# A streaming encoder step on one core: both attentions move from stages of their own into pieces between the expert slots, and the stick-breaking suffix sums accumulate on the logits in PSUM

## The chip, the cores and the metric

One core of one Trainium2 chip (trn2), all arithmetic in fp32. The metric is the device time of one execution in microseconds (us). Engines: PE is TensorE's matmul, PEld its weight load, DVE is VectorE, ACT is ScalarE, POOL is GpSimd, SP is SyncE, which here only issues transfers.

## The reference

1024 prompt rows (8 tiles of 128) and 8 x 16 sample rows (a ninth tile), width 1024. Per layer, cut to what matters:

```
h = rmsnorm(x);  q, k, v, gates = h @ w_in
o_sb  = stick-breaking attention, 8 heads x 64:
          log_keep    = where(mask, -softplus(z), 0)
          log_between = reverse cumsum(log_keep) - log_keep
          weight      = where(mask, exp(log_sigmoid(z) + log_between), 0)
o_sw  = sliding-window softmax, 8 query / 2 key heads x 64, sinks, ALiBi
o_mem = softmax over 256 memory tokens, 4 heads x 128
x += (sum_b gate_b * (o_b @ w_o_b)) @ w_out
x += experts(rmsnorm(x)):  8 heads x top 16 of 16384 single-neuron experts,
       sum over 128 slots of g * gelu(u[idx] . x) * v[idx]
```

The sample tile also attends to caches: 128 past rows of keys and values per sequence for both attentions, and 256 memory rows.

## The kernel before

It has four blocks with a barrier between them. Line numbers are those of the profile.

`project` (lines 81 to 427) normalises the tiles, multiplies them with eight blocks of weights (ksb, vsb, kvsw, qsw, qm, mk, mv, qsb) and leaves queries, keys and values of all nine tiles in SBUF. SP issues the weight loads and the outputs in one written order; a load waits for the block two before it.

`stick` (430 to 672) is the stick-breaking attention: 38 steps, one for each pair of a query tile and a key tile up to the diagonal, and two for the samples. A step is 1024 columns wide (8 heads x 128). PE writes the logits to PSUM; ACT takes Abs, a copy, Exp and Ln (590 to 595), DVE makes the softplus (637), POOL keeps the running sum `later` (612), PE multiplies the softplus by a triangle and `later` by minus ones (531, 533), DVE adds that to the copied logits (651), ACT takes the Exp (581), PE multiplies with the values (552). Line 574 names one activation table set by hand ahead of it, `natural_log_exp_and_others`.

`windows` (675 to 938) is the sliding-window and the memory attention: 27 units (9 tiles, two key heads and the memory), each a softmax over 4 x 256 columns, three in flight. The sample tile's cached keys are transposed on PE there. Outputs of both attentions go to a scratch in DRAM.

`experts` (1020 to 1645) works tile by tile through 128 slots: POOL gathers 128 rows of 8 KB for each slot (1254) into a ring of ten; two slots are a batch (64 a tile, 576 in all). For a batch DVE takes two dot products (1618), ACT the Gelu (1457), DVE the product `wgt` (1624), ACT the diagonal matrices (1468), and PE adds two products of 512 columns to the accumulator (1375). Of tiles with a number in `SIDES`, that many slots of eight go to POOL instead: ACT scales the row (1473) and POOL adds it (1265). Between the batches every engine also does pieces of the `Front` of the next group of tiles: gates and output projections (1298, 1308, tanh 1403, mix 1564), `w_out` (1323), the norm, the expert queries (1346), the key scores (1360), and for the group's first tile the top-k (1489 to 1513) in three pieces a head; the top-k of a later tile is done between the batches of the tile ahead of it. `Front` gives each kind of piece its steps (tau); `paces()` spreads the steps of the next front over the batches of the present group, and `advance(i)` lets each engine do the steps of batch i. Every engine runs its own instructions in the order written, so a piece that waits holds up the batch behind it. Before the first tile, the front of group 0 runs alone up to its first head. The groups are tiles 0 to 1, 2 to 4 and 5 to 8.

```
for q in range(NB):                                   # ScalarE, one batch
    act.wait_ge(dots, m * NB + q + 1)
    nc.scalar.activation(act_[:, c], hid[:, c], ACT.Gelu_apprx_tanh).then_inc(gelus, 1)
    advance(1 + m * NB + q)
    act.wait_ge(weights, m * NB + q + 1)
    ...
```

## Time and profile before

| | us |
|---|---|
| median of 3 runs (4420.18 to 4424.81) | 4423.85 |
| the profiled execution, its own time | 4421.1 |
| its span, first to last instruction | 4419.2 |
| before the first expert slot | 1147 |
| the expert slots of the nine tiles | 3272 |

The span is what the views divide up; the profiled execution's own time is 1.9 us longer. PEclk is TensorE's granted clock as a share of 2.4 GHz. A stretch is named by its first and last microsecond from the span's start. The first tile starts at 1147 us with line 1610.

### The profile page before, as it was taken

Reading aid. Unit: us, or ns where it says so; the run is one execution under the profiler, and the core shown is the slowest. Engines: PE = TensorE matmul, PEld = TensorE weight load, DVE = VectorE, ACT = ScalarE, POOL = GpSimd, SP = SyncE. Lnnn points to the kernel's source line nnn. Section 1 sums busy time; section 2 is a strip of 40 time slices with the busy share of each in tenths; the row PEclk is TensorE's granted clock in tenths of the full one; section 3 lists DMA queues with packets and bytes.
Section 4 is the critical chain, followed back from the end, with each engine's and each line's share of the span. In section 5 each row is a group of like instructions: output and inputs, shape, how many; then the busy total and the mean of one; then the engine's idle time right before and its main releaser. Section 6 shows DMA issues by size and latency. Waiting matters only on the chain.

```text
span 4419.2 us, 34952 instructions
## 1 busy us (share of the span) xinstructions
PE 3611.0 (82%) x11113; PEld 1885.0 (43%) x11113; DVE 2811.9 (64%) x6038; ACT 1235.3 (28%) x2663; POOL 1836.7 (42%) x1477
## 2 busy tenths in 40 slices
PE   7999798989768797867898878996787777787777
PEld 4545457778534345432333335442233233233222
DVE  2130541821698965886996997687677676676554
ACT  2111772620332233332223224333111112112111
POOL 0000340000366576656666666666433333333332
PEclk9999996989889999988999999998899999999999
DMA  3202102234799899989999999999999999999998
GB/s 123 69 25 80 30 1 86 84 122 162 293 351 391 319 405 421 396 333 421 421 419 421 412 420 415 422 411 409 421 421 421 417 412 418 415 413 414 421 421 354
DMA packets 249160, 1415.44 MB, mean 320 GB/s; under 512 B 26624, under 2 KB 59648, under 8 KB 95872
## 3 DMA queue, kind: packets, MB, share of 16 engines
q0 software_dynamic: 165888, 1208.03, 66.6%
q1 hardware_dynamic: 83088, 205.18, 12.6%
q8 instruction: 88, 1.44, 0.1%
q14 instruction: 96, 0.79, 0.0%
HBM read 1374.85 MB, written 39.19 MB: 320 GB/s over the span
## 4 chain that ended last, share of the span: by engine, by line
DMA 23%; POOL 18%; DVE 13%; PE 12%; issue 11%; ACT 2%; POOLq 0%; SPq 0%; ACTq 0%; DVEq 0%
DMA ring<-in_experts_dram,idx 22%; POOL side L1265 10%; POOL ring L1254 8%; PE ps L1375 7%; DVE ring L1618 5%; PE ps L1298 2%; PE ps L1323 1%; DVE wgt L1624 1%; PE ps L1346 1%; PE ps L1308 1%; ACT diag L1468 1%; DVE hot L1507 1%; DVE hot L1510 1%; DVE e L1512 1%; DVE flat L1503 0%
## 5 line engine op out<-in xcount | busy, mean ns | idle before, releaser
L1375 PE MATMUL ps<-ring,diag 128*128 128x512 f32 x3520 | 1792.9, 654 | 688.4 <-ACT diag L1468 667.1
L1254 POOL DMA_INDIRECT ring<-in_experts_dram,idx x1152 | 1096.1, 952 | 1905.9 <-PE ps L1375 1334.5
L1618 DVE CUSTOM_DVE_ANT_0 ring<-ring,ps 128x1024 f32<-128x1024 f32 x1152 | 1381.7, 1217 | 556.1 <-DMA ring<-in_experts_dram,idx 548.7
L1375 PEld LDWEIGHTS ps<-ring,diag 128*128 128x128 f32 x3520 | 695.3, 206 | 1693.2 <-ACT diag L1468 948.7
L1265 POOL TENSOR_TENSOR side<-side,ring 128x1024 f32<-128x1024 f32 x272 | 640.8, 2356 | 42.6 <-ACT ring L1473 37.4
L1457 ACT ACTIVATE act_<-hid 128x2 f32<-128x2 f32 x576 | 117.1, 203 | 1773.5 <-DVE hid L1618 1772.8
L1468 ACT ACTIVATE diag<-const,wgt 128x128 f32<-128x128 f32 x880 | 319.4, 395 | 482.8 <-DVE wgt L1624 480.2
L1298 PE MATMUL ps<-hx,wbuf 128*128 128x256 f32 (+2 forms) x1152 | 403.1, 495 | 13.3 <-DMA hx<-hT_scratch 13.1
L1624 DVE TENSOR_TENSOR wgt<-act_,gw 128x2 f32<-128x2 f32 x576 | 240.9, 418 | 124.9 <-ACT act_ L1457 121.6
L1473 ACT ACTIVATE ring<-ring,wgt 128x1024 f32<-128x1024 f32 x272 | 308.4, 1134 | 0.0
L1298 PEld LDWEIGHTS ps<-hx,wbuf 128*128 128x128 f32 x1152 | 225.6, 196 | 184.5 <-issue 119.3
L301 PE MATMUL ps<-w_qkv,hT 128*128 128x512 f32 (+1 forms) x720 | 283.5, 550 | 1.3 <-DVE mhT L395 1.3
L1346 PE MATMUL ps<-hx,wbuf 128*128 128x256 f32 (+2 forms) x768 | 264.4, 493 | 12.2 <-ACT mixn L1426 11.0
L610 POOL COPY later<-sp 128x1024 f32<-128x1024 f32 x9 | 9.3, 1036 | 478.9 <-DVE sp L643 475.5
L1346 PEld LDWEIGHTS ps<-hx,wbuf 128*128 128x128 f32 x768 | 149.7, 196 | 129.7 <-issue 96.3
L1308 PE MATMUL ps<-o_x,wbuf 128*128 128x256 f32 (+2 forms) x576 | 204.1, 491 | 0.0
L301 PEld LDWEIGHTS ps<-w_qkv,hT 128*128 128x128 f32 x720 | 134.1, 190 | 131.0 <-issue 125.4
L637 DVE SCALAR_TENSOR_TENSOR sp<-ps,za 128x1024 f32<-128x1024 f32 x38 | 46.5, 1224 | 193.2 <-ACT za L595 193.2
L404 DVE TENSOR_REDUCE nrm<-stage 128x4 f32<-128x512 f32 (+2 forms) x29 | 16.3, 561 | 237.9 <-ACT stage L347 237.9
L1308 PEld LDWEIGHTS ps<-o_x,wbuf 128*128 128x128 f32 x576 | 111.4, 193 | 84.4 <-issue 58.5
L1323 PE MATMUL ps<-wbuf,mixn 128*128 128x256 f32 x576 | 129.8, 382 | 1.6 <-DVE mixn L1564 1.6
L1323 PEld LDWEIGHTS ps<-wbuf,mixn 128*128 128x128 f32 x576 | 110.6, 192 | 29.0 <-issue 15.1
(187 smaller groups left out, 3096.6 us busy)
## 6 DMA issues: line engine op xcount, KB each, us to landing
wbuf<-in_w_gate_o_dram SPq DMA_DIRECT2D x72, 768.0 KB, 8.3
wbuf<-in_w_q_dram SPq DMA_DIRECT2D x24, 1024.0 KB, 9.0
ring<-in_experts_dram,idx POOLq DMA_INDIRECT x1152, 16.0
wbuf<-in_w_out_dram SPq DMA_DIRECT2D x12, 1024.0 KB, 8.9
w_qkv<-in_w_in_dram SPq DMA_DIRECT2D x5, 2048.0 KB, 8.0
o_x<-o_scratch SPq DMA_DIRECT2D x9, 768.0 KB, 25.2
s<-s_scratch SPq DMA_DIRECT2D x6, 1024.0 KB, 11.6
hT_scratch<-hT SPq DMA_DIRECT2D x9, 512.0 KB, 7.0
```

The lines of the kernel that those rows point to most:

```text
L301: last = nc.tensor.matmul(ps[:, bank(u), 0:n], src[:, k, t * P:(t + 1) * P], w[:, c % 2, k, 0:n], start=(k == 0), stop=(k == KC - 1))
L1254: i = nc.gpsimd.indirect_dma_start(out=ring[:, j % RING, :], out_offset=None, in_=A["experts"], in_offset=bass.IndirectOffsetOnAxis(ap=idx ...
L1265: nc.gpsimd.tensor_tensor(side[:, m % 2], side[:, m % 2], ring[:, j % RING, DM:2 * DM], ALU.add).then_inc(side_done, 1)
L1298: last = nc.tensor.matmul(ps[:, 4 + u % 2, 0:N].rearrange("p (i t) -> p i t", t=P), w[:, k * P:(k + 1) * P], hx[:, 0:n, k, :], start=(k == ...
L1308: last = nc.tensor.matmul(ps[:, 6 + u % 2, 0:N].rearrange("p (i t) -> p i t", t=P), w[:, k * P:(k + 1) * P], o[:, 0:n, b, k - KC, :], star ...
L1323: last = nc.tensor.matmul(ps[:, 4 + x % 4, 0:2 * P], mixn[:, k * N + i * P:k * N + (i + 1) * P], w[:, k * 2 * P:(k + 1) * 2 * P], start=(k ...
L1346: last = nc.tensor.matmul(ps[:, 4 + x % 2, 0:N].rearrange("p (i t) -> p i t", t=P), w[:, c:c + P], hx[:, 0:n, k, :], start=(k == 0), stop= ...
L1375: last = nc.tensor.matmul(acc[:, h, :], diag[:, (by_pe(j) - 1) % 4, :], ring[:, j % RING, DM + h * HB:DM + (h + 1) * HB], start=(j % SLOTS ...
L1468: last = nc.scalar.activation(diag[:, d % 4, :], ident, ACT.Copy, scale=wgt[:, j % SLOTS:j % SLOTS + 1])
L1473: nc.scalar.activation(v, v, ACT.Copy, scale=wgt[:, j % SLOTS:j % SLOTS + 1]).then_inc(scaled, 1)
L1618: last = nc.vector.tensor_tensor_reduce(out=u, in0=u, in1=xp, scale=1.0, scalar=0.0, op0=ALU.mult, op1=ALU.add, accum_out=hid[:, j % SLOTS ...
L1624: nc.vector.tensor_tensor(wgt[:, c], act_[:, c], gw[:, m % 2, c], ALU.mult).then_inc(weights, 1)
```

## The change

`stick` and `windows` go. `project` also writes everything that they took from SBUF to scratches in DRAM: the normalised rows (nine transfers of 512 KB, before in `stick`), keys, values and three kinds of queries, and the memory's. `Front` now begins with the attentions of its own group and goes on with the gates. Groups are three tiles each. The stick-breaking steps are halves of 512 columns (four heads); group 0 has 12, group 1 has 30, group 2 has 34. Their logits stay in one of three PSUM banks, and the suffix sums are accumulated onto them there, so that the copy (591) and the add (651) go; `later` is kept on DVE instead of POOL. The window units have one set of PSUM banks instead of two. Keys and values come in again a step at a time through rings of three; the bias, the window's and the memory's keys and values come in when the group's stick-breaking part is done, and the gate weights and `hx` when its windows are done, since all of them share one working area. The caches' keys are given to the kernel already transposed. The hand-named table set goes. Steps have costs, and `paces()` spreads the costs, at most two steps a batch. `advance` moves ahead of the accumulation on PE, and behind `wgt` and the diagonals on DVE and ACT. Tiles 2 to 5 now give four slots of eight to POOL (before three in tiles 2 to 4, none in tile 5).

With the numbers of the file, group 0's front runs alone for 136 steps, to its first head, and ends at batch 22 of tile 0. Group 1's stick-breaking steps take batch 22 of tile 0 to batch 3 of tile 1 (46 batches, 29 of which compute logits, one of them of two halves), its windows go on to batch 18 of tile 1, its gates to batch 11 of tile 2, the rest to batch 55 of tile 2. Group 2's stick-breaking steps take batches 0 to 52 of tile 3 (53 batches, 34 with logits), its windows go on to batch 16 of tile 4, its gates to batch 10 of tile 5, the rest to batch 55 of tile 5.

```diff
-GROUPS = ((0, 1), (2, 3, 4), (5, 6, 7, 8))
-PARTS = (2, 3, 4)
-SIDES = (4, 4, 3, 3, 3, 0, 0, 0, 0)
+GROUPS = ((0, 1, 2), (3, 4, 5), (6, 7, 8))
+PARTS = (2, 3, 3)
+SIDES = (4, 4, 4, 4, 4, 4, 0, 0, 0)
 def project(nc, A, S, small_dram, D):
...
+                for t in range(NT):
+                    if kind == "ksb":
+                        sp.dma_start(D["k"][t].rearrange("p (j t) -> p j t", j=4), cols("ksbT", t)).then_inc(spilled, 16)
+                    elif kind == "vsb":
...
+                if t == 1 and c >= 1:
+                    ns += spill(c - 1)
+                if t == 4 and c == 0:
+                    sp.wait_ge(h_done, NX)
+                    for i in range(NT):
+                        sp.dma_start(D["hT"][i], hT[:, :, i * P:(i + 1) * P]).then_inc(spilled, 16)
+                    ns += NT
...
-def stick(nc, A, S, hT_d):
...
-def windows(nc, A, S, wide_dram, o_d):
...
 class Front:
...
+        self.steps_ = []
+        b = 1
+        for i, t in enumerate(GROUPS[g]):
+            kbs = list(range(t, -1, -1)) if t < ST else [ST, None]
+            for k, kb in enumerate(kbs):
+                self.steps_.append((i, t, kb, k == 0, k == len(kbs) - 1, b))
+                b += 2
...
+        self.zscore, self.soft, self.suffix, self.values = at(0), at(1), at(2), at(6)
+        self.plain = at(2, lambda x: not x[3])
+        self.least, self.dexp, self.mask = (at(lag, lambda x: x[3]) for lag in (2, 3, 4))
+        self.late = at(3, lambda x: not x[4])
+        self.okeep = {x[5] + 8: k for k, x in enumerate(self.steps_) if x[4]}
...
+                self.wins.append((i, t, c, b))
+                b += 2 if c < 2 else 3
...
+        self.wscore, self.wfront, self.wexp, self.wnorm = wat(0), wat(1), wat(2), wat(3)
+        self.wturn = {x[3] + 4 + k: (u, k) for u, x in enumerate(self.wins) for k in range(2)}
+        self.wvalues, self.wkeep = wat(6), wat(7)
...
+            c = 0.8
+            c += 4.5 * (tau in self.zscore or tau in self.suffix)
+            c += 2.0 * (self.win_at + 2 <= tau < self.gate_at)
+            c += 10.3 * n / 4 / Y * (tau in self.unit)
+            c += 3.5 * (tau in self.out)
+            c += 3.4 * n / 4 * (tau in self.query) + 1.0 * (tau in self.top)
...
 def paces():
...
+            goal = total * min(1.0, (i + 1) / (ticks - 8))
+            n = 0
+            while at < len(left) and (n < 2 and spent + left[at] / 2 <= goal or i >= ticks - 9):
+                spent += left[at]
+                at += 1
+                n += 1
+            out.append(n)
...
         @block.sync
...
+                    if tau in f.zscore:
+                        k, p = f.zscore[tau]
+                        if p == 1 and k + 3 < f.nkeys:
+                            sp.wait_ge(z_done, f.half(k, 1) + 1)
...
+                    if tau == f.win_at:
+                        sp.wait_ge(st_kept, f.tiles0 + n)
+                        sp.dma_start(bias.rearrange("p h k -> p (h k)"), wide_dram[:, 0:BW]).then_inc(bias_in, 16)
+                        first = 0 if g else 1
+                        for src, dst in ((0, kswT), (1, vsw)):
+                            v = sw_d[f.base - 1 + first:f.base + n, :, src].rearrange("t p c -> p t c")
+                            sp.dma_start(dst[:, first:n + 1], v).then_inc(win_in, 16)
+                        sp.dma_start(mkT.rearrange("p h m -> p (h m)"), mem_d[:, 0]).then_inc(win_in, 16)
+                        sp.dma_start(mv.rearrange("p k m -> p (k m)"), mem_d[:, 1]).then_inc(win_in, 16)
...
+                    if tau in f.mul:
+                        k = f.mul[tau]
+                        for b in range(2 * k + 2, 2 * k + 4):
+                            sp.wait_ge(mul_done, b - 1)
+                            if b < DB:
+                                sp.dma_start(kmem[:, b % 2], A["cache_mem_kT"][b]).then_inc(km_in[b % 2], 16)
+                            else:
+                                load_vm(b - DB)
...
+                    if tau == f.gate_at:
+                        sp.wait_ge(w_kept, f.win1)
+                        for i in range(2):
+                            load(f, i)
+                        for i in range(n):
+                            sp.dma_start(hx[:, i], hT_d[f.base + i]).then_inc(h_in, 16)
...
         @block.tensor
...
+                            pe.wait_ge(minned if f.steps_[k3][3] else weighed, f.sort(k3, p3) + 1)
...
+                        pe.wait_ge(sp_ready, x + 1)
+                        z = ps[:, 4 + x % 3, :]
+                        last = nc.tensor.matmul(z, tri, sps[:, x % 3], start=False, stop=True, skip_group_check=True)
+                        if not first:
+                            pe.wait_ge(latered, f.lates(k - 1, p) + 1)
+                            last = nc.tensor.matmul(z, negones, later[:, p], start=False, stop=True, skip_group_check=True)
+                        last.then_inc(sums, 1)
...
             for m in range(NT):
                 for q in range(NB):
-                    if q == 0:
-                        advance(1 + m * NB)
+                    advance(1 + m * NB + q)
                     accumulate(m, q)
-                    if q:
-                        advance(1 + m * NB + q)
...
         @block.scalar
...
+                        a = za[:, x % 2]
+                        nc.scalar.activation(a, ps[:, 4 + x % 3, :], ACT.Abs).then_inc(absd, 1)
+                        act.wait_ge(absd, x + 1)
+                        nc.scalar.activation(a, a, ACT.Exp, scale=-1.0).then_inc(zexped, 1)
+                        act.wait_ge(zexped, x + 1)
+                        nc.scalar.activation(a, a, ACT.Ln, bias=1.0).then_inc(logd, 1)
+                    if tau in f.dexp:
+                        k, p = f.dexp[tau]
+                        w = wts[:, f.half(k, p) % 5]
+                        act.wait_ge(minned, f.sort(k, p) + 1)
+                        nc.scalar.activation(w, w, ACT.Exp).then_inc(dexped, 1)
+                    if tau in f.plain:
+                        k, p = f.plain[tau]
+                        x = f.half(k, p)
+                        act.wait_ge(sums, x + 1)
+                        if x >= 5:
...
                     nc.scalar.activation(act_[:, c], hid[:, c], ACT.Gelu_apprx_tanh).then_inc(gelus, 1)
-                    advance(1 + m * NB + q)
                     act.wait_ge(weights, m * NB + q + 1)
...
                             nc.scalar.activation(v, v, ACT.Copy, scale=wgt[:, j % SLOTS:j % SLOTS + 1]).then_inc(scaled, 1)
+                    advance(1 + m * NB + q)
...
         @block.vector
...
+                    if tau in f.least:
+                        k, p = f.least[tau]
+                        x = f.half(k, p)
+                        dve.wait_ge(sums, x + 1)
+                        if x >= 5:
+                            dve.wait_ge(pv, x - 4)
+                        nc.vector.tensor_scalar(wts[:, x % 5], ps[:, 4 + x % 3, :], 0.0, None, ALU.min).then_inc(minned, 1)
+                    if tau in f.late:
+                        k, p = f.late[tau]
+                        x = f.half(k, p)
+                        dve.wait_ge(sums, x + 1)
+                        if f.steps_[k][3]:
+                            nc.vector.tensor_copy(later[:, p], sps[:, x % 3]).then_inc(latered, 1)
+                        else:
+                            dve.wait_ge(latered, f.lates(k - 1, p) + 1)
+                            nc.vector.tensor_tensor(later[:, p], later[:, p], sps[:, x % 3], ALU.add).then_inc(latered, 1)
...
+                        sp_ = sps[:, x % 3]
+                        nc.vector.scalar_tensor_tensor(out=sp_, in0=ps[:, 4 + x % 3, :], scalar=0.0, in1=za[:, x % 2],
+                                                       op0=ALU.max, op1=ALU.add).then_inc(sp_raw, 1)
...
+    A["cache_kT"] = give("cache_kT", kc.reshape(DB, P, 4, 2, HD).transpose(3, 4, 0, 2, 1).reshape(P, DB, 4, P))
```

## Rows read from the trace of the kernel before

**Rows 1.** The page, part 1: busy us (share of the span) xinstructions of each engine.
```profile
PE 3611.0 (82%) x11113; PEld 1885.0 (43%) x11113; DVE 2811.9 (64%) x6038; ACT 1235.3 (28%) x2663; POOL 1836.7 (42%) x1477
```

**Rows 2.** Stretches before the first expert slot: us, engines' busy us, PEclk, DMA share, GB/s.
```profile
0.00:429.00 429.00, 402.63 (x1189) 214.41 (x1189) 83.05 (x189) 71.98 (x172) 0.55 (x6) 0.98 0.19 68
429.00:715.00 286.00, 246.68 (x1731) 150.59 (x1732) 122.48 (x102) 191.50 (x199) 99.19 (x47) 0.90 0.11 32
715.00:951.00 236.00, 204.73 (x1243) 182.01 (x1242) 119.78 (x210) 94.60 (x279) 0.00 (x0) 0.77 0.28 92
951.00:1080.00 129.00, 127.76 (x576) 111.10 (x576) 16.54 (x40) 12.87 (x26) 0.00 (x0) 0.98 0.48 165
1080.00:1118.00 38.00, 31.54 (x146) 27.35 (x147) 6.78 (x15) 5.92 (x9) 0.00 (x0) 0.96 0.61 211
1118.00:1147.00 29.00, 29.00 (x148) 25.85 (x147) 12.54 (x54) 6.40 (x13) 1.14 (x1) 1.00 0.46 156
```

**Rows 3.** The expert slots, one stretch for each tile: tiles 0 to 5, and 8.
```profile
1147.00:1600.00 453.00, 339.80 (x889) 178.34 (x888) 395.90 (x871) 140.88 (x255) 272.87 (x194) 0.88 0.92 359
1600.00:2024.00 424.00, 320.70 (x938) 174.86 (x936) 307.33 (x623) 137.24 (x259) 273.91 (x193) 0.91 0.97 392
2024.00:2376.00 352.00, 306.48 (x666) 130.30 (x667) 297.06 (x615) 103.28 (x210) 241.97 (x180) 0.95 1.01 420
2376.00:2741.00 365.00, 311.63 (x808) 157.01 (x806) 300.19 (x626) 105.52 (x213) 232.59 (x174) 0.94 1.01 416
2741.00:3103.00 362.00, 296.02 (x731) 134.26 (x731) 273.73 (x602) 125.86 (x252) 237.78 (x178) 0.89 1.01 415
3103.00:3431.00 328.00, 251.05 (x515) 101.67 (x513) 235.40 (x593) 61.11 (x196) 124.07 (x131) 0.93 1.01 421
...
4088.00:4419.00 331.00, 241.93 (x520) 94.09 (x520) 171.21 (x324) 58.12 (x195) 112.84 (x121) 0.99 0.96 399
```

**Rows 4.** Line 1624 alone, one a batch: us, busy us (batches), PEclk, DMA share, GB/s.
```profile
1328.00:1600.00 272.00, 30.81 (x40) 0.94 0.92 361
1801.00:1929.00 128.00, 14.20 (x16) 0.95 0.90 343
1608.00:1706.00 98.00, 15.21 (x16) 0.98 1.01 421
...
3107.00:3395.00 288.00, 9.03 (x56) 0.92 1.01 421
```

**Rows 5.** A transfer of 512 KB beside the expert slots: KB, median us to landing.
```profile
xrow<-xn_scratch SPq DMA_DIRECT2D x9, 512.0 KB, 11.3
```

**Rows 6.** Groups of instructions: xcount | busy us, mean ns | idle before. ScalarE.
```profile
L1468 ACT ACTIVATE diag<-const,wgt 128x128 f32<-128x128 f32 x880 | 319.4, 395 | 482.8 <-DVE wgt L1624 480.2 <-PE ps L1375 2.3
L1473 ACT ACTIVATE ring<-ring,wgt 128x1024 f32<-128x1024 f32 x272 | 308.4, 1134 | 0.0
L1457 ACT ACTIVATE act_<-hid 128x2 f32<-128x2 f32 x576 | 117.1, 203 | 1773.5 <-DVE hid L1618 1772.8
L355 ACT ACTIVATE vsb<-ps 128x512 f32<-128x512 f32 x9 | 5.4, 597 | 56.3 <-PE ps L301 56.3
```

**Rows 7.** ScalarE in order of time around an Exp between two other functions.
```profile
1140.88 1.28 ACT L1449 ACT_TABLE_LOAD   x1
1142.17 0.22 ACT L1449 ACTIVATE best<-best 128x16 f32<-128x16 f32 x1
1142.41 1.28 ACT L1457 ACT_TABLE_LOAD   x1
```

**Rows 8.** The view of rows 6, VectorE.
```profile
L1618 DVE CUSTOM_DVE_ANT_0 ring<-ring,ps 128x1024 f32<-128x1024 f32 x1152 | 1381.7, 1217 | 556.1 <-DMA ring<-in_experts_dram,idx 548.7 <-DVE idx L1513 1.4 <-DVE gw L1533 0.6
L637 DVE SCALAR_TENSOR_TENSOR sp<-ps,za 128x1024 f32<-128x1024 f32 x38 | 46.5, 1224 | 193.2 <-ACT za L595 193.2
```

**Rows 9.** Line 1624: duration ns min/median/max, first and last start.
```profile
L1624 DVE TENSOR_TENSOR wgt<-act_,gw x576: 146/160/2989, 1164.7 to 4410.3; 128x2 f32<-128x2 f32 x192
```

**Rows 10.** A stretch late in tile 1, in the columns of rows 3.
```profile
1929.00:2024.00 95.00, 45.58 (x77) 16.11 (x75) 70.51 (x141) 28.68 (x53) 62.64 (x44) 0.75 0.98 393
```

1071 lines of the change are left out of this document (528 added, 543 removed).

## The prediction

> **What bounds the kernel now.** PE is busy 82% of the span [rows 1], so I read where in the span, by stretches. Until 1147 us no expert is gathered: 429 us of projections, 286 of stick-breaking, 236 of windows, 196 of group 0's front, with the DMA share at 0.11 to 0.61 [rows 2]. Then nine tiles take 3272 us. From tile 2 on (tiles 6 and 7 are like tile 5) the DMA share reads 1.01 at 415 to 421 GB/s: gathers bound these tiles, and a batch without pieces costs 288 / 56 = 5.1 us [rows 3, 4]. Tiles 0 and 1 are not at that bound (0.92 and 0.97). Where pieces of the top-k and of the front meet, DVE sets the pace: 128 / 16 = 8.0 us a batch at 1801 to 1929 us, 272 / 40 = 6.8 at 1328 to 1600, against 6.1 at 1608 to 1706, where the DMA is full again [rows 4]. PE is seldom what ends last there: tile 2 took 352 us with 306 of PE. So the change moves work from a place where transfers are idle to one where they bound. It pays if the pieces fit under 5.1 to 5.7 us a batch, and one engine that doesn't fit stops all, since each works in order.
>
> **Before the first slot.** Projections, 429 us: the spill of the memory queries now stands in SP's order ahead of the last block's weights (8 us, about one landing of [rows 5]), the last nine spills follow the last product (11), and the first loads must land (11.3, of which some 2 were there): +28, between +10 and +45. The other spills lie under PE's work, at a DMA share of 0.19 [rows 2]. Without that cover their 19 MB would cost some 45 us.
>
> Stick-breaking of group 0, 12 halves: ACT takes four passes of 512 columns, 0.60 each [rows 6], and two table loads of 1.28 [rows 7], 5.0 in all. That gives 60, and the turns between three tiles 16: 76 us. At the old rate of 286 / 38 = 7.5 a step, six steps would be 45. That and 110 are the ends.
>
> Windows of group 0, nine units on one set of banks: product (2, my estimate), bias and maximum on DVE (1.22 each for 1024 columns [rows 8], plus 0.5 for small ones, an estimate), four Exp at 0.6 at most [rows 6]: 7.4 a unit, 67 for nine, 10 until the last is out, 11 for the loads [rows 5]: 88. A third of 236 would be 79; I keep up to 120.
>
> Gates to first head: three tiles in place of two. 129 x 1.5 = 194; the 38 grow to 52 (28 of it scale, 10 don't); the 29 to 38; and 11 for weights that are asked for only when the windows are done: 295.
>
> Sum: 457 + 76 + 88 + 295 = 916 where 1147 was, **-231 us**.
>
> **In the slots: stick-breaking.** Take ACT in a batch with one logits half. Gelu 0.20, one diagonal 0.40, one scaled row 1.13, Abs, Exp, Ln and the weights' Exp 0.60 each: 4.1 us [rows 6]. To that come table loads. In [rows 7] an Exp between two other functions cost two loads of 1.28, with 0.01 us between load and neighbour. The change runs Exp, Ln, Exp, Gelu in a circle and no longer names a table set. No row shows whether Exp and Ln then share a set. I take four loads, 5.1 us, because the kernel before had to name the joint set by hand; two is the other end. So 9.3 us, and a batch at a tile's start needs two or three loads: 8.7 on average, 8.4 in group 2. The next Gelu stands behind the pieces on ACT, `wgt` behind Gelu (0.15 to 2.99 us, [rows 9]) and the diagonals behind that, so about 0.6 of ACT's idle time comes on top: 9.3 and 9.1. DVE in such a batch has two dots (2.6 with their read-outs), `wgt` 0.5, a softplus and a `later` of half the 1.22 each with waits, 2: about 5 [rows 8], which is hidden, but with the third piece of a head's top-k (8) it is 13. The ring of ten covers five batches once, then the slow rate stands.
>
> Group 1: 46 batches, 29 x 9.3 + 17 x 5.6 + 8 heavy pieces x 4 = 397. Before, 46 x 6.8 = 313 [rows 4]. **+84**. Group 2: 53 batches, 34 x 9.1 + 19 x 5.6 + 32 = 448; before at tile 3's 365 / 64 = 5.7 [rows 3], 302. **+146**. The copy, the add and POOL's `later` that go were hidden in the old stage's time, already removed above.
>
> By the Trainium skill (ScalarE: Activation LUTs, What ACT_TABLE_LOAD costs) a switch also takes a drain and costs 2.66 us in all; the some 310 new loads would add 430 us to my sum. The trace disagrees with that part: [rows 7] leave no room for it.
>
> **Windows.** DVE's 5.3 us a unit (1.22 three times, a copy and small ones 1.6) x 9 = 48, over 15 batches 3.2, on 3.1 of the slots and 1.7 of the top-k: 8.0 against 6.1, +28. In group 2 over 28 batches 6.5 against 5.7, +22. The sample's 16 memory transfers go two deep: six times PE waits some 11 us [rows 5] in four or five batches, with `accumulate`, and behind it POOL's gathers, queued: +25, between 5 and 70. Window and gate loads start one batch ahead of use, four places, 11 less 6 each: +20.
>
> **The rest of the front** spreads further. Tile 5 had none (328); at tile 1's full-DMA rate of 6.1 [rows 4] it takes 378: +50. Tile 2 +30, tile 4 +20, tile 1 +5; tiles 6 to 8 as before. One more slot of eight on POOL in tiles 2 to 4, and four in tile 5, is in these rates: tile 1 ran so, with POOL at 274 of 424 [rows 3]. New bytes (keys, values, bias, caches, some 36 MB) are 86 us at 420 GB/s, but lie in batches that are now slower than the DMA.
>
> `advance` behind `wgt` and the diagonals takes the front's waits out of PE's way, but DVE and ACT do the same work in a batch: I take nothing, and 30 either way for the ends.
>
> Sum: 84 + 146 + 28 + 22 + 25 + 20 + 105 = **+430**. The profiled execution took 4421.1 (span 4419.2), 2.7 below the median of 4423.85, under 0.1%. 4421 - 231 + 430 = **4620 us**. A measurement of this kernel can tell about 0.2%, 9 us, from no change.
>
> **Rivals.**
> A. *Everything fits under the gathers* (the other side: faster). If a batch with stick-breaking comes to about 6 us, the ring evens it out and bytes alone bound the slots. That needs ACT's loads nearly gone. The nine slot stretches times their DMA shares are some 3210 (two are not shown) [rows 3]; with 86 of new bytes, 10 of start and 60 for tile 0's top-k, 3366; with 916, 4282. For it: 0.92 to 1.01 in [rows 3]. Against it: 4.1 us plus even two loads is 6.7. 0.14.
> B. *Two loads a batch.* The batch falls by 2.2 us in 63 batches, less where DVE's heavy pieces rule, 115; and group 0's halves need none, 31: 4474. For it: nothing in [rows 7] excludes it. The Trainium skill (ScalarE activation tables: per-element evaluation and per-set limits, Table sets in the compiler and the runtime) says that loads are placed by the greedy longest run, which would choose the joint set here; no run so far shows it. 0.2, with a quarter of it below 4412.
> C. *PE falls to its lower clock and the loads queue.* At full clock 288 products of 256 columns took 128 us [rows 2], 0.44 each, so 512 columns 0.87. A stick-breaking batch has 0.9 of logits, 0.9 of values, 1.7 of sums and 1.7 of accumulation, 5.2 us, half of a batch of 9.3. Half busy late in tile 1 (46 of 95 us, [rows 10]) the granted clock read 0.75. At 1.2 GHz it is 10.4, over ACT's 9.3: 63 x 1.5 = 95, and the load waits double, 45: 4760. 0.14.
> D. *The change doesn't do what it says*: the stages go and the steps are issued as written; less than 0.01.
> My forecast has 0.52.
>
> **Numbers.** The range is 4400 to 4760: it leaves out A (0.14) and the far end of C, and takes in B and the unsure terms above (-20/+17 before the stick-breaking, -31/+34, -9/+32, -20/+45 for the sample's loads). Faster: A 0.14, a quarter of B, 0.05, and 0.01: 0.20. Same 0.04. Slower 0.76.
>
> **What would show it.** The first copy of `xrow` (line 1610 before) at 905 to 930 us. ACT_TABLE_LOAD: some 330 in place of about 50 (two a batch: some 200), three or four between Gelus in tiles 0 and 3. Tiles 0 to 5: some 530, 440, 382, 530, 415, 380 us, and 328 after that. ACT busy over 7 us a batch in tile 3, DMA share 0.7 to 0.8 there, the diagonals waiting for `wgt` and Gelu behind ACT's own pieces. The forecast is wrong if tile 3 stays under 430 us with its DMA share over 0.9 (A), if loads are half as many (B), or if PE is over 90% busy there at a clock near 0.5 (C).

## The result, and the profile after

The changed kernel takes 4815.9 us (median of 4 runs, 4812.2 to 4826.9) beside 4422.0 of the kernel before: ratio 1.0897, 95% interval 1.0874 to 1.092. The forecast was 4620 with a range to 4760: the direction was right, the loss 394 us and not 196.

The page of the changed kernel, parts 1 and 2: busy us of each engine, then tenths in 40 slices (120 us each). It answers to [rows 1].

```profile
PE 3634.3 (75%) x10561; PEld 1921.8 (40%) x10561; DVE 2936.3 (61%) x6134; ACT 1702.6 (35%) x3098; POOL 2011.2 (42%) x1542
...
ACT  2111510237774423333488733323332211111111
POOL 0000000164444366766645434466766633333332
PEclk9997799987787789999788776699999799989999
DMA  4323023587766599999977666699999899999998
```

DMA is no longer full in slices 9 to 13 and 20 to 25, counted from 0. Those are the two places where attention goes between the slots. PE was busy about as long as before (3634 us, 3611 before), in a span that is 399 us longer. The first copy of `xrow` stands at 939.6 us, where it was 1147: the front of the kernel gives 207 us back, and the slots take 3878 us, where they took 3272. The nine tiles take 533, 487, 411, 583, 461, 420, 324, 327 and 331 us.

To see which pieces are slow, I count batches by the start of the Gelu, and cut the slots where the kind of piece changes (us / batches). A cut can lie a batch to either side, where one batch has pieces of both kinds. "Start" is the time of the first Gelu, "stick" is stick-breaking, and 1 and 2 are groups 1 and 2. "Rest" is the output projection, the queries and the key scores; the last 200 batches have no pieces.

| kernel | start | stick 1 | windows 1 | gates 1 | rest 1 | stick 2 | windows 2 | gates 2 | rest 2 |
|---|---|---|---|---|---|---|---|---|---|
| after | 943 | 378/44 | 192/16 | 352/57 | 340/52 | 450/52 | 298/29 | 362/58 | 317/45 |
| e1 joint table | 921 | 336/44 | 192/16 | 350/57 | 342/52 | 405/52 | 300/29 | 358/58 | 318/45 |
| e2 no Exp, Ln | 921 | 327/44 | 197/16 | 349/57 | 346/52 | 355/52 | 296/29 | 354/58 | 315/45 |
| e3 price 5.3 | 942 | 375/40 | 261/28 | 339/53 | 332/49 | 425/46 | 360/47 | 323/52 | 287/39 |
| e4 early loads | 943 | 393/43 | 178/20 | 341/56 | 332/51 | 458/51 | 290/32 | 345/57 | 310/44 |
| e5 sums first | 940 | 483/44 | 192/16 | 370/57 | 365/52 | 589/52 | 311/29 | 366/58 | 327/45 |
| e6 spread | 940 | 399/43 | 189/19 | 361/56 | 339/51 | 454/51 | 300/32 | 361/57 | 304/44 |
| e7 sides 3 | 944 | 377/44 | 192/16 | 352/57 | 325/52 | 438/52 | 290/29 | 358/58 | 300/45 |
| e9 no side, tiles 0, 3 | 944 | 346/44 | 199/16 | 352/57 | 341/52 | 432/52 | 282/29 | 362/58 | 318/45 |
| e10 no side | 942 | 349/44 | 174/16 | 399/57 | 356/52 | 426/52 | 283/29 | 401/58 | 309/45 |
| e13 by stage | 921 | 305/43 | 171/20 | 333/56 | 318/51 | 355/51 | 261/32 | 337/57 | 290/44 |

Over the 5.95 us that a batch of tiles 0 to 5 took on average before (2284 / 384 by [rows 3]), the two stick stretches have 257 us too much, the two windows stretches, with only 45 batches, 222, the two rests 80, and the gates 30.

The table loads on ScalarE in the changed kernel (line, engine, instruction, count | busy us, mean ns | idle before; the largest groups):

```profile
L1415 ACT ACT_TABLE_LOAD x111 | 142.4, 1283 | 1.9
L1314 ACT ACT_TABLE_LOAD x76 | 97.5, 1283 | 1.3
L1312 ACT ACT_TABLE_LOAD x71 | 91.1, 1283 | 1.3
L1326 ACT ACT_TABLE_LOAD x47 | 60.3, 1283 | 0.8
```

They stand before the Gelu, the Ln, the first Exp and the weights' Exp: four to a plain stick batch, 361 in all. Exp and Ln didn't share a set.

The engines' busy times in stick 1, stick 2, windows 1 and windows 2 of the changed kernel, in the columns of [rows 3]:

```profile
1113.00:1490.00 377.00, 257.07 (x767) 127.82 (x765) 253.59 (x567) 299.73 (x375) 187.16 (x131) 0.79 0.72 265
2375.00:2825.00 450.00, 317.70 (x1100) 168.69 (x1100) 282.83 (x592) 343.61 (x431) 227.32 (x158) 0.80 0.73 272
1491.00:1683.00 192.00, 101.65 (x352) 64.61 (x352) 110.86 (x224) 78.39 (x162) 68.11 (x49) 0.72 0.53 196
2826.00:3124.00 298.00, 186.15 (x697) 126.28 (x697) 167.29 (x304) 101.41 (x204) 121.53 (x84) 0.67 0.67 250
```

In the stick stretches ScalarE is busiest, at 76 to 80%. In the windows stretches no engine is busy for more than 63%, and the DMA share is 0.53 and 0.67: there the time is in waits. In windows 1 they are (who, line, for whom | us in total, times, longest):

```profile
POOL ring L1002 <- PE ps L1284: 118.0, 12, 19.9
ACT act_ L1415 <- DVE hid L1676: 56.3, 10, 25.8
DVE work L1566 <- PE ps L1136: 30.8, 2, 22.0
DVE wgt L1681 <- ACT act_ L1415: 30.3, 17, 7.3
ACT work L1354 <- PE ps L1154: 29.1, 9, 4.9
PEld ps L1136 <- ACT work L1345: 23.2, 4, 10.2
PEld ps L1136 <- DMA work<-mem_scratch: 21.4, 1, 21.4
```

GpSimd waits 118 of 192 us to be allowed to gather, for the expert sums on TensorE; those stand behind window scores (line 1136), which wait for ScalarE's Exp of the window before (1345), once for a load. One engine's wait is thus every engine's.

The chain of work that ended last shows how one window waits for the next. From it, the load and the step from the first window's scores to the second's (start us, us, what):

```profile
1493.64 20.98 DMA work<-mem_scratch
1514.66 3.79 PE ps L1136 x8
1518.48 1.24 DVE work L1566
1519.74 1.23 DVE mx L1572
...
1521.43 1.12 DVE ring L1676
1522.56 1.13 DVE ring L1676
1523.97 1.79 DVE wgt L1681
1526.10 1.13 ACT ring L1428
1527.25 1.28 ACT L1341
1528.75 1.97 ACT work L1345 x8
1530.77 3.79 PE ps L1136 x8
```

Scores, bias and maximum take 6.3 us, the Exp 2.0. Between them stand 7.8 us, most of it the batch's own two dot products, the weight product (stretched to 1.79 us) and a side row, and a table load. That makes 16.1 us from one window's scores to the next.

### The profile page after: what moved, and what is told of

Same layout as the page of the kernel before. It is cut to its first block, busy times and chain, and to the rows that moved or that the text cites. A ratio compares the mean times of both kernels' runs of the same rounds, so it can differ in the third digit from the quotient of the medians.

```text
span 4817.7 us, 34691 instructions
## 1 busy us (share of the span) xinstructions
PE 3634.3 (75%) x10561; PEld 1921.8 (40%) x10561; DVE 2936.3 (61%) x6134; ACT 1702.6 (35%) x3098; POOL 2011.2 (42%) x1542
## 4 chain that ended last, share of the span: by engine, by line
POOL 32%; issue 25%; DMA 13%; PE 12%; DVE 5%; ACT 2%; SPq 0%; POOLq 0%; ACTq 0%; DVEq 0%
POOL side L1013 18%; POOL ring L1002 14%; DMA ring<-in_experts_dram,idx 12%; PE ps L1284 4%; PE ps L1211 3%; DVE ring L1676 2%; PE ps L1217 1%; PE ps L1232 1%; PE ps L1136 1%; PE ps L1255 1%; DMA work<-mem_scratch 1%; PE ps L1170 1%; ACT diag L1423 1%; ACT work L1345 0%; PE ps L1154 0%
## 5 line engine op out<-in xcount | busy, mean ns | idle before, releaser
L1284 PE MATMUL ps<-ring,diag 128*128 128x512 f32 x3072 | 1637.4, 674 | 702.7 <-ACT diag L1423 674.2
L1013 POOL TENSOR_TENSOR side<-side,ring 128x1024 f32<-128x1024 f32 x384 | 904.8, 2356 | 8.1
L1428 ACT ACTIVATE ring<-ring,wgt 128x1024 f32<-128x1024 f32 x384 | 434.9, 1133 | 0.0
L1211 PE MATMUL ps<-work 128*128 128x384 f32 x1152 | 399.7, 496 | 41.2 <-DMA work<-hT_scratch 41.2
L1211 PEld LDWEIGHTS ps<-work 128*128 128x128 f32 x1152 | 224.3, 195 | 218.6 <-issue 47.4
L1255 PE MATMUL ps<-work 128*128 128x384 f32 x768 | 270.3, 500 | 8.3 <-ACT work L1376 8.3
L1255 PEld LDWEIGHTS ps<-work 128*128 128x128 f32 x768 | 152.3, 199 | 136.5 <-issue 58.8
L1217 PE MATMUL ps<-o_x,work 128*128 128x384 f32 x576 | 199.0, 489 | 0.0
L1051 PE MATMUL ps<-o_x,work 64*128 64x128 f32 x592 | 107.3, 342 | 102.5 <-ACT work L1326 80.7
L1051 PEld LDWEIGHTS ps<-o_x,work 64*128 64x128 f32 x592 | 91.7, 240 | 170.8 <-ACT work L1326 106.0
L1217 PEld LDWEIGHTS ps<-o_x,work 128*128 128x128 f32 x576 | 110.6, 192 | 86.3 <-issue 19.0
L1232 PE MATMUL ps<-work 128*128 128x256 f32 x576 | 131.7, 386 | 10.9 <-DVE work L1622 10.9
```

Of the source, the lines that this page charges most:

```text
L1013: nc.gpsimd.tensor_tensor(side[:, m % 2], side[:, m % 2], ring[:, j % RING, DM:2 * DM], ALU.add).then_inc(side_done, 1)
L1211: last = nc.tensor.matmul(ps[:, 4 + u % 2, 0:N].rearrange("p (i t) -> p i t", t=P), w[:, k * P:(k + 1) * P], hx[:, 0:n, k, :], start=(k == ...
L1217: last = nc.tensor.matmul(ps[:, 6 + u % 2, 0:N].rearrange("p (i t) -> p i t", t=P), w[:, k * P:(k + 1) * P], o[:, 0:n, b, k - KC, :], star ...
L1255: last = nc.tensor.matmul(ps[:, 4 + x % 2, 0:N].rearrange("p (i t) -> p i t", t=P), w[:, c:c + P], hx[:, 0:n, k, :], start=(k == 0), stop= ...
L1284: last = nc.tensor.matmul(acc[:, h, :], diag[:, (by_pe(j) - 1) % 4, :], ring[:, j % RING, DM + h * HB:DM + (h + 1) * HB], start=(j % SLOTS ...
L1428: nc.scalar.activation(v, v, ACT.Copy, scale=wgt[:, j % SLOTS:j % SLOTS + 1]).then_inc(scaled, 1)
```

## The experiments

Each states its edit against the changed kernel. Times are device us; single runs where no spread is given. The changed kernel and those timed four times spread by up to 0.3%.

**e1, e2: the table loads.**

```diff
+            def joint():
+                if table[0] != "joint":
+                    nc.scalar.preload_act_table_set("natural_log_exp_and_others")
+                    table[0] = "joint"
...
+                        joint()        # ahead of Abs, of the diagonal's Exp and of the weights' Exp
```


> The joint table of Exp and Ln is named once before each run of stick-breaking operations on ScalarE, nothing else. Theory 1 (table loads make ScalarE the bound of the two stick-breaking stretches that stand in place of expert slots): loads fall from four to two a batch, so the trace's total of 361 falls to about 210; 99 batches at 8.7 to 8.9 us come down to between 7.0 and 7.5 us, ScalarE's busy time falls by about 150 x 1.28 = 190 us, and the time falls by 130 to 170 us, to 4650 to 4690 us. Theory 2 (the round trips between the engines and the fourth side transfer on GpSimd set those stretches): loads fall as much, ScalarE idles longer, and the time falls by less than 50 us, to above 4765. The stretches with windows, at 8.2 to 11.9 us a batch, don't change by either theory, since they have no Ln.

4713.2 (4706.4 to 4719.2), ratio to before 1.0661 (1.0643 to 1.068): -103. The two groups of loads that are left for stick-breaking are the Gelu's and that of the joint set:

```profile
L1427 ACT ACT_TABLE_LOAD x111 | 142.4, 1283 | 2.0
L1304 ACT ACT_TABLE_LOAD x76 | 97.5, 1283 | 1.4
```

and stick 1 as a stretch, in the columns of [rows 3]:

```profile
1091.00:1427.00 336.00, 244.77 (x767) 120.73 (x765) 263.27 (x567) 233.45 (x323) 187.46 (x131) 0.82 0.80 298
```

```diff
-                        nc.scalar.activation(a, a, ACT.Exp, scale=-1.0).then_inc(zexped, 1)
+                        nc.scalar.activation(a, a, ACT.Copy, scale=-1.0).then_inc(zexped, 1)
...
-                        nc.scalar.activation(a, a, ACT.Ln, bias=1.0).then_inc(logd, 1)
+                        nc.scalar.activation(a, a, ACT.Copy, bias=1.0).then_inc(logd, 1)
...
-                        nc.scalar.activation(w, w, ACT.Exp).then_inc(dexped, 1)
+                        nc.scalar.activation(w, w, ACT.Copy, scale=1e-3).then_inc(dexped, 1)
...
-                        nc.scalar.activation(wts[:, x % 5], ps[:, 4 + x % 3, :], ACT.Exp).then_inc(weighed, 1)
+                        nc.scalar.activation(wts[:, x % 5], ps[:, 4 + x % 3, :], ACT.Copy, scale=1e-3).then_inc(weighed, 1)
```


> Leaves out the Exp and the Ln of the stick-breaking (Copy in their place, of the same shapes), so no table is loaded in its pieces. Theory 1: the stick stretches come down to the next bound, 6.3 to 6.8 us a batch, and the time falls by 190 to 240 us against the changed kernel, to 4575 to 4625. Theory 2: hardly more than with the joint table, both under 50 us. If this run gains no more than the joint table does, two loads a batch cost nothing and another limit stands at 7 us or more.

4646.8: -169. Two loads a batch gone gave 41, 45 and 22 us in stick 1, stick 2 and ahead of the slots; the next two 10, 50 and 0. Theory 1 holds with a smaller size (103 and 169 us, where it said 130 to 170 and 190 to 240): ScalarE lost 66 us of busy time in stick 1 and the stretch 41 (busy in 69% of it, from 80%), so waits filled over a third of what was freed. In stick 1 something else bounds from 7.4 us a batch on; in stick 2 ScalarE was still the limit.

**e3, e4, e6: why the windows take 10 to 12 us a batch.**

```diff
-            c += 2.0 * (self.win_at + 2 <= tau < self.gate_at)
+            c += 4.5 * (self.win_at + 2 <= tau < self.gate_at)
```


> The planner's price of a step in the windows rises from 2.8 to 5.3, so that about one such step goes in a batch where two went. Theory A (two dependent steps a batch on one set of PSUM banks: the chain from scores over the shift, Exp, two turns and values crosses engines more often than a batch has room for): windows batches fall from 9.4 us to 6.5 to 7.2 us while there are twice as many, so the stretch costs the same or up to 60 us less in all; the gates behind it get more units a batch. Time between 4740 and 4830. Theory B (the excess is waits for loads that start at the first window step): the excess stays where it is, at the entry, and the time stays within 20 us of 4816, or rises up to 60 us as the gates are crowded.

4826.8: +11. The windows go from 12.0 to 9.3 and from 10.3 to 7.7 us a batch, not to the 6.5 to 7.2 of theory A, and there are 75 such batches: the two stretches grow from 490 to 621 us. The denser stick stretches give little of that back (375 us for 40 batches where 44 took 378, and 425 for 46 where 52 took 450). The sum doesn't tell the theories apart.

```diff
-        b = self.win_at + 2
+        b = self.win_at + 10
...
-        self.gate_at = g0 = max(self.wkeep) + 1
+        self.gate_at = max(self.wkeep) + 1
+        g0 = self.gate_at + 8
```


> Eight empty steps are put between the place where the loads of the windows (and of the gates) are issued and the first step that uses them, in each of the three groups, so the loads land in four batches' time. Theory B (waits for these loads are what the windows cost over their 6.1 us a batch): the 20.5 us wait of the first window product and its like go, four of them: time falls by 60 to 90 us, of which the prelude gives 0. Theory A: the waits were hidden behind other work or small, and the time changes by -20 to +20 us (empty steps cost almost nothing but crowd the rest).

4775.8: -40, between the two theories. Loads issued too late are part of it. The batch of the first window scores still took 17.7 us, with 11.3 us of wait for a load of the memory's: eight empty steps are four batches of 3 to 5 us, and the loads needed longer than that.

```diff
-                b += 2 if c < 2 else 3
+                b += 3
```


> A window's scores start three steps behind the last one's, not two, so they no longer share a step with the Exp that frees their banks (18 + 9 more steps in the first and third of the groups alike, at the planner's 2.8 each). Theory A2: windows batches fall from 12.0 and 10.3 us to 8.5 or less with some 30 per cent more of them, windows together from 490 to 400 to 450 us, the time by 30 to 70 us. Theory A1 or loads: the same sum of stalls over more batches, and the time within 20 us of 4816.

4839.9: +24, but the windows stretches are as long as before, with three batches more in each (189 for 16 + 3, 300 for 29 + 3). That fits a length set by their own dependent steps, but it doesn't hold for more batches (e3 above, e16 and e17 below). The batches gained there are no gain, since the stick stretch, one batch shorter, and gates 1 took longer.

**e5: the order on TensorE.**

```diff
-                    advance(1 + m * NB + q)
-                    accumulate(m, q)
+                    accumulate(m, q)
+                    advance(1 + m * NB + q)
```


> TensorE takes the batch's expert sums ahead of the front's steps, not behind them (for q = 0 too). In the windows stretch of the changed kernel GpSimd's gathers wait 108.8 us in 178 for exactly these sums, since they stand behind window products that wait for ScalarE's Exp. Theory A1 (the order on TensorE holds the ring): the windows fall from 12.0 and 10.3 us a batch to 9 or less, and the time falls by 60 to 120 us. Theory A2 (the windows' own chain, scores -> shift -> Exp -> next scores on one pair of banks, is the length of a batch, whatever TensorE does first): the waits only move, and the time is within 30 us of 4816. In the stick stretches the scores come later in a batch; if ScalarE waits for them, those stretches rise by 0.2 to 0.5 us a batch (20 to 50 us) by either theory.

5134.4: +318, a miss of both theories. The windows did not fall, and the stick stretches rose by 105 and 138 us. The waits in stick 1 of this run, the longest first:

```profile
POOL ring L1002 <- PE ps L1284: 273.5, 37, 10.8
PEld ps L1284 <- ACT diag L1423: 230.5, 43, 10.7
PE ps L1284 <- ACT diag L1423: 202.5, 39, 10.5
DVE wgt L1681 <- ACT act_ L1415: 182.3, 44, 10.5
ACT work L1310 <- PE ps L1051: 108.0, 29, 4.8
```

The sums wait for the diagonals, these for `wgt` and Gelu, and Gelu for the last pieces on ScalarE; now the logits wait behind the sums, and ScalarE for the logits (108 us in 29 batches). The two chains of a batch, which ran side by side, follow each other. The order that the change gives TensorE is a condition for its stick pieces.

**e7, e9, e10: the side rows.** Ahead of these I looked at VectorE between GpSimd's additions. In time order, in stick 2 of the changed kernel:

```profile
2512.33 2.35 POOL L1013 TENSOR_TENSOR side<-side,ring 128x1024 f32<-128x1024 f32 x1
...
2512.80 1.91 DVE L1681 TENSOR_TENSOR wgt<-act_,gw 128x2 f32<-128x2 f32 x1 [5.53 <-ACT act_ L1415]
2514.63 0.41 DVE L1454 TENSOR_TENSOR cand<-v 128x256 f32<-128x256 f32 x1
...
2518.17 3.35 DVE L1465 TENSOR_TENSOR hot<-partf,const 128x512 f32<-128x512 f32 x1
2518.61 2.35 POOL L1013 TENSOR_TENSOR side<-side,ring 128x1024 f32<-128x1024 f32 x1
```

`wgt`, 128 x 2 elements and 0.16 us long when free, ends 0.03 us after GpSimd's addition (2514.68).

```diff
-SIDES = (4, 4, 4, 4, 4, 4, 0, 0, 0)
+SIDES = (4, 4, 3, 3, 3, 3, 0, 0, 0)          # e7
+SIDES = (0, 4, 4, 0, 4, 4, 0, 0, 0)          # e9
+SIDES = (0, 0, 0, 0, 0, 0, 0, 0, 0)          # e10
```


> Tiles 2 to 5 send three value rows of eight over ScalarE and GpSimd, not four, so TensorE takes five of eight. If GpSimd's part (4 x 3.3 us per 8 slots) was what slowed tiles 2 to 5: ScalarE and GpSimd have less to do and TensorE 1.6 us more per 8 slots; the third stick stretch, bound by ScalarE, falls by 1.13 us in four batches (15 us in 52 batches), and the time by 10 to 30 us. If TensorE bounds the gates (2.40 GHz, about 5.3 us busy a batch in tile 2): tiles 2 and 5 rise by 0.4 us a batch each and the time stays or rises by 20 to 40 us.

> Tiles 0 and 3, where the stick-breaking goes between the slots, send no value row over ScalarE and GpSimd (0 of 8 for 4 of 8); the tables stay as they are. In the changed kernel VectorE's product of the weights, 0.16 us when free, took 1.39 us on average in the 187 batches in which it ran beside a side addition of GpSimd (2.35 us each), and up to 2.99; all such stretched operations together 382 us, before 250. Theory S (side work fills ScalarE's queue and holds VectorE): per batch ScalarE loses one scaling (1.13) and gains one diagonal (0.40), and a stall of about 1 us goes: 128 batches, 0.7 to 1.5 us each, time 90 to 190 us less, 4625 to 4725. Theory T (table loads alone bound these stretches; the side work is hidden): ScalarE's 0.73 us a batch on 96 stick batches still counts, 40 to 70 us less, and no more. Against both: TensorE gets 0.99 us a batch more; if it bound, the tiles would rise.

> No side transfer in any tile. Theory S: tiles 0 and 3 as in the run with sides only out of them; in tiles 1, 2, 4 and 5 the windows stretch gets shorter too (0 to 1.5 us a batch of 45), but the gates at 6.2 us a batch, of which TensorE is busy 5.2 to 5.4, rise to 6.4 to 7.0, 100 to 150 us for 210 batches. Time between 4680 and 4800, above the run that keeps the sides there. If the stall of VectorE bound the gates too, they would fall below 6.2.

e7 4762.0 (-54), e9 4741.2 (-75), e10 4803.6 (-12, at the edge of the 4680 to 4800 that were said). e7 gained more than expected (10 to 30): 16 and 18 us in the rests, 12 in stick 2, and 9 and 4 in windows 2 and gates 2. The two rests, after first, then e7:

```profile
2035.00:2375.00 340.00, 257.66 (x771) 144.38 (x769) 274.01 (x550) 112.11 (x214) 221.01 (x155) 0.88 0.98 396
3486.00:3803.00 317.00, 239.15 (x741) 137.94 (x739) 243.66 (x514) 100.42 (x194) 196.84 (x138) 0.90 0.95 379
```
```profile
2036.00:2361.00 325.00, 264.79 (x817) 148.98 (x816) 252.80 (x552) 102.78 (x215) 187.25 (x142) 0.93 1.00 411
3447.00:3747.00 300.00, 251.32 (x792) 144.66 (x790) 224.19 (x516) 92.43 (x194) 169.08 (x126) 0.94 0.99 401
```

VectorE lost 41 us of busy time over both, with the same operations: that was waiting counted as work. e9 lies between its two theories (40 to 70 and 90 to 190 us). In it the top-k batches ahead of stick 1 fell by 20 us, stick 1 by 32, stick 2 by 19. e10 shows the other side: gates at 7.0 us a batch for 6.2, since the rows go to TensorE instead, and windows 1 fall by 18 us. That it is the addition that holds `wgt` is shown by the row of e10, which has no side row at all (min/median/max ns), beside 160/161/2993 in the changed kernel:

```profile
L1681 DVE TENSOR_TENSOR wgt<-act_,gw x576: 160/161/225, 941.7 to 4792.8; 128x2 f32<-128x2 f32 x192
```

**e8, e11, e12, e13: together.** e8 is e1, e4, e5 and e6. e11 is e1 and e4 with 3 side rows of eight in tiles 0 to 5; e12 the same with 0, 0, 3, 0, 3, 3. In e13 the side rows go by stage:

```diff
+    if 0 <= j // BATCH < 85 or 192 <= j // BATCH < 275:       # stick-breaking, windows
+        return False
     return j % 8 in SIDE_AT[SIDES[j // SLOTS]]                 # 3 in tiles 0 to 5
```


> Joint table, loads eight steps early, sums first on TensorE and three steps between scores, together. The joint table gave -103 us and the early loads -40 us alone; if they add up with -30 to -120 us of the two others, the time is 4550 to 4640 us. It would still be slower than before's 4423, since stick and windows together then still hold 7.5 us a batch against 5.1 where no front runs: if it falls below 4423, the limit was none of the work but only these stalls.

> Joint table, loads eight steps early, and three side rows of eight in tiles 0 to 5. If the single effects add (-103, -40, -54 and some 20 for tiles 0 and 1): 4600. If they overlap, since each frees the same chain: 4640 to 4680. Not below 4560, so still slower than before by 3 per cent or more.

> Joint table, loads eight steps early, and side rows 0, 0, 3, 0, 3, 3 of eight in tiles 0 to 5. Theory S: 40 to 90 us below the same with 3 in all, 4510 to 4590; still above before's 4423, since windows (their chain of 15 to 20 us for each of 18 windows) stay. Below 4423 only if the chain of the windows shortens with the sides too, by more than 5 us a window.

> Joint table, loads eight steps early, and the side rows by stage: none in the batches with stick-breaking or windows (and none before them in tile 0), three of eight in the gates and the rest of tiles 1 to 5. From the run with 0, 0, 3, 0, 3, 3 of eight by tile (4504.9): tile 1's gates, 6.57 us a batch there, return to the 5.96 that they took with three of eight (56 batches, -34), the windows in tile 4 lose their sides (19 batches, 0 to -10), tile 3's last batches change nothing. Time 4460 to 4480 us, still above before's 4423. If the sides' cost in the stick stretches is not local to them (ring credit carried over), 4490 to 4510.

e8 4892.5, a miss (4550 to 4640 said): the loss by the order on TensorE outweighs the rest. e11 4553.7 (-262) and e12 4504.9 (-311) lie just under their ranges. e1, e4 and e7 add up to 197, and some 20 was expected of tiles 0 and 1, so the effects together are more than the sum of the single ones; my reading is that each had covered part of the others. e13 4450.4 (4444.5 to 4454.3; 4460 to 4480 said), ratio to before 1.0067 (1.0047 to 1.0087): 365 of the 394 us are gone, with the same pieces, all still between the slots. Its stick and its windows stretches:

```profile
1062.00:1366.00 304.00, 277.59 (x935) 137.96 (x935) 223.96 (x560) 200.16 (x320) 83.41 (x87) 0.97 0.90 334
2188.00:2542.00 354.00, 342.01 (x1280) 184.28 (x1281) 242.76 (x585) 229.86 (x368) 96.63 (x101) 0.95 0.90 342
1367.00:1538.00 171.00, 127.15 (x443) 72.79 (x442) 109.42 (x252) 70.17 (x174) 37.99 (x38) 0.86 0.71 266
2542.00:2803.00 261.00, 221.44 (x842) 134.26 (x841) 146.90 (x328) 86.06 (x215) 61.83 (x64) 0.84 0.83 319
```

In the stick stretches the DMA share is 0.90 now and TensorE is busy 91 and 97%: the next limit is near. The windows are still waits.

**e14: the tables of the windows.**

```diff
-                            nc.scalar.activation(mx[:, r, 4, :], mx[:, r, 3, :], ACT.Exp)
+                            nc.scalar.activation(mx[:, r, 4, :], mx[:, r, 3, :], ACT.Copy, scale=1e-3)
...
-                            last = nc.scalar.activation(L[:, r, j, :], src[:, j, :], ACT.Exp, bias=mx[:, r, 1, j:j + 1], scale=scale,
+                            last = nc.scalar.activation(L[:, r, j, :], src[:, j, :], ACT.Copy, scale=1e-3,
```


> Leaves out the Exp of the windows (Copy of the same shapes, no bias), so no table is loaded for them: 36 loads of 1.28 us less in the two window stretches, 46 us of ScalarE. Theory A2' (the windows stretch is as long as the dependent chain of its steps, whatever the number of batches: 192 and 298 us): the loads stand in that chain, the bias form may be 0 to 2 us a window shorter, and the time falls by 40 to 70 us, to 4745 to 4775. Theory L (the excess of 220 us over 6.0 us a batch is mostly waits for the windows' own loads): time falls by less than 20 us.

4786.9: -29, between the two theories, of which 15 and 11 in the two stretches. The 34 loads that went hold 44 us, so about 0.6 of their length was on the path, if the Copy itself gained nothing.

**e16, e17: windows over more batches**, on e13, with the price of a window step at 3.5 and 5.0 in place of 2.0 over the 0.8. The batches without side rows end where the windows then end.

> As the run with sides by stage (4450.4), and the planner's price of a window step from 2.8 to 4.3 (65 batches with windows, not 47 to 52; the batches with stick-breaking from 95 to 89). Theory C (a window stretch is as long as the chain of its own steps, DMA share 0.70 and 0.83 there): more batches fit in nearly the same time, the gates and the rest, at a DMA share of 1.01, don't change a batch; 15 batches more in the windows at 2.7 to 4.5 us in place of 5.9 to 6.2: 25 to 45 us less, 4405 to 4425. Rival: every batch that holds a step makes its own round trip (one step a batch cost 9.3 us in the run with the price of 5.3 on the changed kernel), and the time rises by 0 to 30 us.

> The same with the price at 5.8 (82 batches with windows, about one step a batch; 84 with stick-breaking). Theory C: a further 0 to 20 us less than with 4.3, as the stick batches get denser and lose some of it: 4395 to 4425. Rival: 4460 to 4500.

4469.8 (4468.2 to 4474.2) and 4467.5 (4461.2 to 4475.6): 19 and 17 us slower than e13, the rival. Windows 1 go 171/20, 205/24, 205/30, windows 2 261/32, 305/41, 356/52. From e13 to e17 a batch more costs 3.4 and 4.8 us there, near what theory C had. What it had wrong is the stages from which the batches were taken. The two sticks give back 56 us for 10 batches and the two gates some 44 for 10, but the rests only some 12 for 9: rest 2 went 290/44, 289/41, 279/38, so a batch less gives back 1.8 us there and not the 6.6 of the average. Together 30 batches more cost 129 us in the windows and gave back 112 elsewhere: moving batches between stages moves little.

**e15: the kernel before with 3 side rows in tiles 0 and 1.**

```diff
-SIDES = (4, 4, 3, 3, 3, 0, 0, 0, 0)
+SIDES = (3, 3, 3, 3, 3, 0, 0, 0, 0)
```


> The kernel before with three side rows of eight in tiles 0 and 1, not four, nothing else. In its tiles 0 and 1 (7.0 and 6.6 us a batch) VectorE's weight products wait for GpSimd's additions as in the kernel after. Theory S: 64 side additions less in 128 batches at 0.3 to 0.6 us each: 20 to 50 us less, 4375 to 4405. Rival: TensorE bounds tile 0's gates and the time is within 10 us of 4423, or up to 20 above.

4412.3 (10 runs, 4399.1 to 4416.2), ratio 0.9972 (0.996 to 0.9984): 10 us faster, mostly in tile 0 (449 to 431 us in the profiled executions). Smaller than the expected 20 to 50, but it is the one version here that beats both kernels.

## Why the prediction was wrong

**What it had right.** The change moves work from where transfers idle to where they bound. The start, by its terms: projections until the first product of the stick-breaking 460 us (457 said), stick group 0 92 (76), windows 100 (88), gates to the first copy 288 (295), together 940 for 916. Stick group 1 took 385 us over its 46 batches (397 said) and group 2 462 over its 53 (448): four loads a batch, ScalarE as the bound, DMA share 0.72. Rival B's condition is false, and its price was 146 us where naming the set by hand gave 103. The Trainium skill (ScalarE activation tables: per-element evaluation and per-set limits, Table sets in the compiler and the runtime) has the loads placed by the greedy longest run, which I took to choose the joint set; the count of 361 disagrees. The 2.66 us for a switch with its drain, which the Trainium skill gives (ScalarE: Activation LUTs, What ACT_TABLE_LOAD costs), isn't borne out either: 34 loads taken out of the windows gave 26 us there. Rival C had the clock (0.79 in stick 1) but not the bound: TensorE was busy 68% there, and in e13 it runs the same pieces at 0.97, with less waiting. Its sum also takes 1.5 us a batch where 10.4 less 9.3 is 1.1, so 70 us and not 95.

**What failed: the windows term.** "DVE's 5.3 us a unit ... over 15 batches 3.2 ... +28", +22 in group 2, +25 for the sample and +20 for late loads come to 95 us. By the table they cost 227: 192 us in 16 batches (98 at 6.1), and 298 in 29 (165 at 5.7). That is 132 of the 196 us by which the loss was larger than forecast. The term priced work, as if the steps were spread over the batches. What the trace shows is a chain. With one set of banks the kernel starts a window's scores only after the Exp of the window before (`pe.wait_ge(w_exped, U)`; before, with two sets, after the Exp of the window before that). The bias, the maximum and the Exp are queued in program order behind the batch's own work: 16.1 us from scores to scores for the first two windows of windows 1, and 21.0 us for the load ahead of them, where 11.3 was taken. For two of three windows that wait is stricter than the code needs: their Exp reads SBUF, and the banks are free once the bias is added (line 1566). No run tried the looser wait.

In e6 three batches more left the stretches as long as they were; in e3, e16 and e17 each batch more cost 3 to 9 us. The parts of the excess, as the runs give them: loads for the windows and gates issued earlier, 40 us of time, where 20 was said for all four places; table loads, 26, where the term had none; side rows, from three of eight to none, 21 and 26 (from e11, whose windows took 192 and 287 us, to e13). What is left in e13 is 123 us over 5.95 a batch (432 us in 52 batches). I take that for the chain itself, but no run shows it: none gave the windows their second set of banks back, and none separates what the lower clock in these stretches (0.72 and 0.67, in e13 0.86 and 0.84) adds.

**The second failed step.** "One more slot of eight on POOL in tiles 2 to 4, and four in tile 5, is in these rates": the rates came from tile 1 before, where GpSimd was busy 65%, and I asked only whether GpSimd has the time. It costs VectorE instead. [rows 9] had it in plain sight, 146 / 160 / 2989 ns for an operation on 256 elements, and I used it as the scatter of a wait. e7 prices that one row of eight in tiles 2 to 5 at 54 us. It is about half of what tiles 2 and 5 took over the forecast (29 and 40 us; with three rows they are 15 and 19 us shorter), and in tiles 0 and 3 the side rows stand in the stick batches, where the forecast had them as ScalarE's 1.13 us alone; e9, with none there, is 75 us faster.

**A step that was right by luck.** For the order of `advance` I took "nothing, and 30 either way". e5 shows that TensorE's place alone is worth 318 us, 243 of them in the two stick stretches whose terms came out near.

The 394 us of loss are then: four loads a batch and not two, 103 (the forecast had them); side rows, late loads, and their overlap with the first, 263; 28 us remain in e13, with the DMA share at 0.90 in its stick stretches. Nothing in these runs says that moved attention pays: what it saves ahead of the slots (some 230 us in e13) it costs in them, even in e13, where most of what was put beside it by choice is taken away.

## What to carry to other kernels

Price a chain of dependent steps laid between other work by its length too, with what stands before each step in its queue, and not only by its busy time over the batches; look at which engine's operation frees its buffers and what stands behind that in each queue. Read the maximum of an operation's duration beside its median: a tiny operation that takes 3 us is held by another engine, and that engine's "free" time has a price. A changed order of two calls on one engine needs a price as well. Where a function of another table set stands between Exp and Ln, name the joint set by hand and count the loads.

## What the runs showed of the hardware

- VectorE is held while GpSimd adds. In the changed kernel `wgt` took 0.16 us in 389 batches clear of an addition and 1.39 us on average in 187 beside one; small products, shifts and casts of 0.17 to 0.56 us became 1.8 to 2.9 on average. MAX8, FIND_INDEX8, the read-outs, the reduction and the dot product, whose second operand lies in PSUM, kept their length (1.22 us for the dot product in both). The Trainium skill (SBUF — State Buffer, Who interferes with whom) says that a VectorE instruction with two SBUF inputs contends with a GpSimd instruction that reads SBUF, that one in a mode with both ports contends with GpSimd too, and that of the two the one issued first has the shared ports for its whole length while the other "fully blocks". The trace agrees on what is held, and that it is held to the end: all 187 products ended within 0.15 us after their addition. It doesn't show the part on the order: 15 of them had started up to 0.61 us before the addition and were held all the same, and the additions kept their length (2.34 to 2.38 us, and one of 384 at 2.67).
- Exp and Ln that follow each other loaded a table each (1.28 us), unless the joint set was named; then neither loads, and the Exp of the weights behind them doesn't either (76 groups in e1, one load each).
- The granted clock of TensorE was lower where it had more gaps: 0.79 in stick 1 of the changed kernel, busy 68%; 0.92 in e9, busy 85%; 0.97 in e13, busy 91%, for the same pieces and more rows of the sums. A product of 512 columns into the accumulator took 967 ns on average in stick 1 of e5 (clock 0.74) and 758 in that of the changed kernel (0.79).
- A gather landed in a median of 5.5 us in windows 1 of the changed kernel and of 17.7 in its last three tiles, where gathers bound. In these stretches a short landing time went with a DMA share of 0.53, a long one with 0.99.
